# Values held and probabilities streamed in the last two attentions of a two-block transformer kernel

## The chip, the cores and the metric

The kernel runs on one core of one Trainium2 chip. The metric is the device time of one execution in microseconds. Engines are named as in the profile: PE multiplies matrices (PEld loads its stationary operand), DVE, ACT and POOL work on vectors, SP only issues transfers.

## What is computed

The reference applies two transformer blocks to 256 tokens of width 1024, in float32. The first has a dilated attention and a dense causal one, 8 heads each, and a feed-forward part. The second has two layers: a sparse attention of 16 heads (a compressed, a selected and a window branch, each with a gate per token and head), then an attention over key blocks of 16 heads; each layer ends in a mixture of 32 experts and a gated embedding. With 256 tokens all keys are in reach, so selected and window branch are two causal attentions with a linear bias. What the change touches, cut from the reference:

```python
o_s = jnp.einsum('bgrqnl,bgqnld->bgrqd', p_s.astype(v_g.dtype), v_g)
...
o_w = jnp.einsum('bgrqk,bgkd->bgrqd', p_w.astype(vwc.dtype), vwc)
o = gc[..., 0:1] * o_c + gc[..., 1:2] * o_s + gc[..., 2:3] * o_w
...
return o @ w_out
```

```python
pr = jax.nn.softmax(sc, axis=-1)
...
o = (jnp.einsum('bgrqkl,bgrqkld->bgrqd', p_sel, v_g)
     + jnp.einsum('bgrql,bgld->bgrqd', p_own, vo))
return o.transpose(0, 3, 1, 2, 4).reshape(b, MOBA_Q_BLOCK, ATT_DIM)
...
h = h + mix.astype(h.dtype)
```

## The kernel before

The program is written engine by engine: each engine has one list of instructions in an order set by hand, and semaphores join them. Nothing reorders. Weights come through `ring`, eight slots of 512 KB filled by SP; each chunk is split into a high part (a cast on ACT) and a low part (a subtraction on DVE) in `weight_parts` (four of them, `PAIRS`), and a product is three matmuls per chunk and tile: high x high, high x low, low x high (`pe_linear`, L881). An input of such a product is first turned by PE (`pe_turn`, L787), then rounded by ACT into `x_high` and subtracted by DVE into `x_low`.

There are four attentions. The first, `att_a` (8 heads, from about 98 us), and the second, `att_b`, belong to block one. The third, `att_n`, holds 32 heads (for each of four key groups four heads on selected keys, gate 1, then the same four on window keys, gate 2, whose result is added); the fourth, `att_m`, 16 heads. One head has two query tiles: 128 queries against 128 keys, 128 queries against 256 keys, side by side in 384 columns (`SPAN`). Its way:

- scores on PE (`scores_of_four`, L975, four heads at a time, two heads at once on row halves) into banks 0 to 3;
- bias and negated maximum on DVE (L1080, two instructions and two short reads) into `logit`, exponentials with their sum on ACT (L1044) into `prob`, four buffers;
- three transposes on PE (`turn_probs`, L985) into bank 4 or 5, a copy to `probT` (ACT L1053 for even heads, DVE L1089 for odd ones), two buffers;
- values on PE (L996): `probT` is held, 128 columns of values are streamed, three times;
- for four heads, DVE takes the reciprocal of the sums (L1100), multiplies by the gate (L1103), scales the values from the banks into `mix` (L1108) and adds where the core has `add` (L1111).

In the third attention a compressed branch runs along: DVE shifts its scores (`dve_shift_compressed`, L1179 to L1184), ACT exponentiates, DVE weighs (L1193 to L1201), PE turns it at the end and multiplies with `own_values` (L1160) and DVE adds into `mix` (L1208). After each of these two attentions `mix` is turned, split, and multiplied by the output weights (`l_nsa_o`, `l_moba_o`). POOL scales some queries and keys (L950) and clears halves of the turned keys (`clear_keys`, L2004), for which PE waits.

## Time and profile before

| | us |
|---|---|
| median of three runs | 1079.68 (1078.15 to 1079.87) |
| the profiled execution | 1079.15 |
| its span in the profile | 1077.4 |
| third attention, first score to its output projection | 57.39 |
| fourth attention, the same | 28.17 |

What stands outside the span in the profiled execution is 1.75 us. The page of the profile gives each engine's busy share; a window query gives the same for a stretch, and the timeline lists instructions with the idle time before them and what ended it.

### The profile page before, as it was taken

Reading aid. Unit: us, or ns where it says so; the run is one execution under the profiler, and the core shown is the slowest. Engines: PE = TensorE matmul, PEld = TensorE weight load, DVE = VectorE, ACT = ScalarE, POOL = GpSimd, SP = SyncE. Lnnn points to the kernel's source line nnn. Section 1 sums busy time; section 2 is a strip of 40 time slices with the busy share of each in tenths; the row PEclk is TensorE's granted clock in tenths of the full one; section 3 lists DMA queues with packets and bytes.
Section 4 is the critical chain, followed back from the end, with each engine's and each line's share of the span. In section 5 each row is a group of like instructions: output and inputs, shape, how many; then the busy total and the mean of one; then the engine's idle time right before and its main releaser. Section 6 shows DMA issues by size and latency. Waiting matters only on the chain.

```text
span 1077.4 us, 17463 instructions
## 1 busy us (share of the span) xinstructions
PE 1022.7 (95%) x6136; PEld 854.6 (79%) x6136; DVE 766.3 (71%) x1347; ACT 700.9 (65%) x1201; POOL 104.0 (10%) x189
## 2 busy tenths in 40 slices
PE   7998899999998999799999999999989999999998
PEld 6876788999997877787687778767878688778766
DVE  4686557666666667777668788787766768888876
ACT  5665545434445536575588898957666578899955
POOL 9008000000000101000320000000010240000000
PEclk9998999999999999999999999999999999999999
DMA  9871028566654555004439999854324428999950
GB/s 295 287 238 56 1 84 246 181 188 180 193 175 162 157 192 200 1 2 156 176 119 327 332 339 339 305 194 147 127 79 152 180 69 326 336 333 339 334 181 40
DMA packets 106156, 209.25 MB, mean 194 GB/s; under 512 B 7736, under 2 KB 51744, under 8 KB 105824
## 3 DMA queue, kind: packets, MB, share of 16 engines
q1 hardware_dynamic: 103584, 204.04, 55.6%
q0 software_dynamic: 2064, 3.25, 1.1%
q8 instruction: 43, 0.70, 0.3%
q10 hardware_dynamic: 432, 0.99, 0.3%
q14 instruction: 33, 0.27, 0.1%
HBM read 207.19 MB, written 1.06 MB: 193 GB/s over the span
## 4 chain that ended last, share of the span: by engine, by line
PE 83%; DVE 7%; ACT 5%; issue 2%; POOL 2%; DMA 1%; SPq 0%; ACTq 0%; DVEq 0%; POOLq 0%
PE bank L881 21%; PE bank L1638 18%; PE bank L1657 11%; PE bank L1311 8%; PE bank L1321 8%; PE bank L996 4%; PE bank L985 2%; PE bank L975 2%; PE bank L787 2%; PE bank L1679 1%; PE bank L1506 1%; DMA ring<-in_a_w_in 1%; PE bank L1649 1%; PE bank L1468 1%; PE bank L2161 1%
## 5 line engine op out<-in xcount | busy, mean ns | idle before, releaser
L881 PE MATMUL bank<-weight_parts,x_high 128*128 128x512 f32 (+2 forms) x768 | 224.1, 376 | 8.6 <-ACT x_high L851 2.6
L1638 PE MATMUL bank<-expert_high,block_high 128*128 128x256 f32 x560 | 183.4, 328 | 3.3 <-ACT block_low L1586 2.4
L1566 DVE TENSOR_TENSOR expert_low<-expert_w,expert_high 128x1024 fp32r<-128x1024 f32 x140 | 164.6, 1218 | 10.6 <-ACT expert_high L1559 10.4
L881 PEld LDWEIGHTS bank<-weight_parts,x_high 128*128 128x128 f32 x768 | 140.0, 189 | 35.8 <-ACT x_high L851 6.9
L1638 PE MATMUL bank<-expert_high,block_low 128*128 128x256 f32 x560 | 158.1, 282 | 0.0
L902 DVE TENSOR_TENSOR weight_parts<-ring,weight_parts 128x1024 fp32r<-128x1024 f32 (+3 forms) x112 | 121.2, 1103 | 51.7 <-ACT weight_parts L899 51.0
L1638 PE MATMUL bank<-expert_low,block_high 128*128 128x256 f32 x560 | 158.0, 282 | 0.0
L899 ACT CAST weight_parts<-ring 128x1024 fp32r<-128x1024 f32 (+3 forms) x112 | 104.3, 956 | 77.5 <-PE bank L881 58.3
L1559 ACT CAST expert_high<-expert_w 128x1024 fp32r<-128x1024 f32 x140 | 140.1, 1053 | 18.9 <-DMA expert_w<-in_moe_w_up 18.4
L881 PE MATMUL bank<-weight_parts,x_low 128*128 128x512 f32 (+2 forms) x384 | 143.6, 374 | 0.0
L1657 PE MATMUL bank<-expert_w,junk 128*128 128x512 f32 x280 | 131.2, 592 | 0.0
L1638 PEld LDWEIGHTS bank<-expert_high,block_high 128*128 128x128 f32 x560 | 106.8, 191 | 20.4 <-issue 14.3
L1638 PEld LDWEIGHTS bank<-expert_low,block_high 128*128 128x128 f32 x560 | 106.9, 191 | 14.7 <-issue 14.7
L1638 PEld LDWEIGHTS bank<-expert_high,block_low 128*128 128x128 f32 x560 | 106.8, 191 | 0.0
L1311 PE MATMUL bank<-x_high,parts 128*128 128x256 f32 x512 | 97.5, 283 | 0.4 <-DVE x_low L853 0.3
L1321 PE MATMUL bank<-parts,hid_parts 128*128 128x512 f32 x384 | 92.9, 391 | 0.0
L1713 DVE SCALAR_TENSOR_TENSOR arena<-bank,home_w,arena 128x1024 f32 x64 | 82.2, 1284 | 9.3 <-issue 5.6
L1311 PEld LDWEIGHTS bank<-x_high,parts 128*128 128x128 f32 x512 | 82.1, 191 | 2.2 <-issue 0.7
L881 PEld LDWEIGHTS bank<-weight_parts,x_low 128*128 128x128 f32 x384 | 72.4, 189 | 12.8
L1321 PEld LDWEIGHTS bank<-parts,hid_parts 128*128 128x128 f32 x384 | 70.1, 188 | 13.3
L1657 PEld LDWEIGHTS bank<-expert_w,junk 128*128 128x128 f32 x280 | 47.7, 190 | 34.4 <-issue 34.3
L1584 ACT CAST block_high<-sorted_high 128x1024 fp32r (+1 forms) x70 | 73.4, 1051 | 1.8 <-issue 1.0
(357 smaller groups left out, 1699.9 us busy)
## 6 DMA issues: line engine op xcount, KB each, us to landing
expert_w<-in_moe_w_gate SPq DMA_DIRECT2D x70, 512.0 KB, 5.9
expert_w<-in_moe_w_up SPq DMA_DIRECT2D x70, 512.0 KB, 7.3
expert_w<-in_moe_w_down SPq DMA_DIRECT2D x70, 512.0 KB, 5.5
ring<-in_w_ff SPq DMA_DIRECT2D x64, 512.0 KB, 3.9
ring<-in_w_in SPq DMA_DIRECT2D x16, 512.0 KB, 8.7
ring<-in_a_w_in SPq DMA_DIRECT2D x16, 512.0 KB, 6.5
ring<-in_ple_w_gate SPq DMA_DIRECT2D x16, 512.0 KB, 5.5
ring<-in_w_o SPq DMA_DIRECT2D x8, 512.0 KB, 4.1
```

Source lines behind the costliest of these rows:

```text
L881: mm = nc.tensor.matmul(bank[:, j["m"] % 4, 0:n], j["operand"][x][:, 2 * c + kk, at[0]:at[1]], weight_parts[:, number % PAIRS, w, kk * n:( ...
L899: nc.scalar.copy(high, raw_weights).then_inc(weights_high, 1)
L902: nc.vector.tensor_tensor(low, raw_weights, high, ALU.subtract).then_inc(weights_split, 1)
L996: mm = nc.tensor.matmul(bank[:, 6 + t, (n % 4) * P:(n % 4 + 1) * P], probT[:, n % 2, q * P:(q + 1) * P], v[:, kt, at - 64:at + 64], start= ...
L1311: mm = nc.tensor.matmul(bank[:, b, 0:256], parts[:, u % 2, w, k * P:(k + 1) * P], x[:, k, :], start=k == 0 and n == 0, stop=k == KB - 1 an ...
L1321: mm = nc.tensor.matmul(bank[:, 2 * t + half, :], hid_parts[:, u % 2, x, t * P:(t + 1) * P], parts[:, u % 2, w, 2048 + half * 512:2048 + ( ...
L1559: nc.scalar.copy(half_of(expert_high[:, b % 2, :], j), half_of(expert_w[:, b % DEPTH, 0:2048], j)).then_inc(ex_cast, 1)
L1566: nc.vector.tensor_tensor(half_of(expert_low[:, b % DEPTH, 0:2048], j), half_of(expert_w[:, b % DEPTH, 0:2048], j), half_of(expert_high[:, ...
L1584: nc.scalar.copy(block_high[:, b % 2], sorted_high[:, :, ds(at, P)]).then_inc(ex_copied, 1)
L1638: mm = nc.tensor.matmul(bank[:, 4 + b % 2, 0:256].rearrange("p (q n) -> p q n", q=2), x[:, b % 2, k, :], w[:, k], start=k == 0 and n == 0, ...
L1657: mm = nc.tensor.matmul(bank[:, 2 * (b % 2) + half, :], hidTs[:, b % 2, :], expert_w[:, b % DEPTH, 2048 + half * 512:2048 + (half + 1) * 5 ...
L1713: v.scalar_tensor_tensor(out=here, in0=bank[:, 2 * (b % 2):2 * (b % 2) + 2, :].rearrange("p b n -> p (b n)"), scalar=share_of, in1=here, o ...
```

## The change

- In the last two attentions the shares (reciprocal of the sum, times gate) are made per pair of heads, and POOL multiplies the probabilities by them, in place, before they are turned.
- `values` now holds 64 columns of values and streams `probT` (256 and 128 columns); two heads write the two halves of the partitions of one bank, which is then one chunk of the mixed rows, already turned. Selected and window branch of a pair accumulate in the same bank, the compressed branch is added there by two more matmuls (`joined`).
- ACT rounds a finished pair into `x_high`, DVE subtracts into `mixed_low`; the turns of `mix` and the additions after the loop go. The output weights are read in the matching row order (`rows_by_chunk`).
- `probT` has four buffers. The first splits of the output weights move into the last group of heads.
- In the first attention the turn of queries and keys moves into `l_va`, ahead of its third chunk, and DVE's two roots behind its copy of `l_va`; in the third, DVE spreads `own_values` before it takes the compressed scores; ahead of the fourth, `l_v`'s splits move ahead of root and scaling, and half of the queries is turned inside `l_v`.
- POOL no longer clears halves of turned keys.
- SP's transfer of the embedding weights waits for the last pair instead of the last mix.

```diff
                 c = chunk(lambda x: x[:, 0:2 * width].rearrange("p (k n) -> p k n", k=2),
-                          w.rearrange("(p k) n -> p k n", k=k)[:, kp:kp + 2, c0:c0 + width], 1,
+                          w.rearrange("(k p) n -> p k n" if rows_by_chunk else "(p k) n -> p k n", k=k)[
+                              :, kp:kp + 2, c0:c0 + width], 1,
                           (weights_split, number + 1))
...
-    t_mix2 = turn(mix, KB, [(x_high, None, x_low)])
-    l_nsa_o = linear(a["a_w_out_2"][0], KB, D_MODEL, x_parts, h, "add")
+    l_nsa_o = linear(a["a_w_out_2"][0], KB, D_MODEL, mixed_parts, h, "add", rows_by_chunk=True)
...
             for c, number in enumerate(group[0]["splits"]):
+                if turn_ahead is not None and group[0] is jobs[0] and c == 2:
+                    pe_turn(pe, turn_ahead)
                 if turned_by and group[0] is jobs[0]:
                     wait_turned(pe, turned_by[c:c + 1])
+                if pairs_mixed is not None and group[0] is jobs[0]:
+                    pe.wait_ge(pair_mixed, pairs_mixed + 2 * c + 2)
...
+    def pe_pairs(pe, s, compressed=False):
+
+        first, here, count = s["first"], s["heads"], len(s["heads"])
+        pairs = pairs_of(s)
+
+        def turn_probs(j):
+            n = first + j
+            pe.wait_ge(weighed, s["first_weighed"] + j + 1)
+            if j >= 2:
+                pe.wait_ge(*probT_of(n - 2))
+            if compressed and j == 6:
+                pe.wait_ge(cT_ready, 1)
+            for q in range(3):
+                mm = nc.tensor.transpose(bank[:, 4 + n % 2, q * P:(q + 1) * P], prob[:, n % 4, q * P:(q + 1) * P],
+                                         ident)
+            mm.then_inc(probs_turned, 1)
...
+        def values(m):
+            x = pairs[m]
+            n = first + 2 * m
+            for i in range(2):
+                pe.wait_ge(*probT_of(n + i))
+            if x["opens"] and x["freed"]:
+                pe.wait_ge(pair_mixed, x["freed"])
+            joined = compressed and x["closes"]
+            for kt, lo, hi in ((0, 0, 2 * P), (1, 2 * P, 3 * P)):
+                for i, head in enumerate(x["heads"]):
+                    v, at = head["v"]
+                    mm = nc.tensor.matmul(bank[64 * i:64 * i + 64, x["bank"], P * kt:2 * P], v[:, kt, at:at + 64],
+                                          probT[:, (n + i) % 4, lo:hi], start=x["opens"] and kt == 0,
+                                          stop=x["closes"] and kt == 1 and not joined, skip_group_check=True)
+            if joined:
+                half = x["chunk"] // 4
+                cols = slice(x["chunk"] % 4 * P, x["chunk"] % 4 * P + P)
+                for t in range(TILES):
+                    mm = nc.tensor.matmul(bank[:, x["bank"], t * P:(t + 1) * P], own_values[:, half, cols],
+                                          cT[:, 2 * half + t, :], start=False, stop=t == 1, skip_group_check=True)
+            mm.then_inc(pair_made, 1)
+
+        scores_of_four(pe, first, here[0:4])
+        if compressed:
+            pe.wait_ge(c_scored, KV_HEADS)
+        for j in range(0, count, 4):
+            if j + 4 < count:
+                scores_of_four(pe, first + j + 4, here[j + 4:j + 8])
+            turn_probs(j)
+            turn_probs(j + 1)
+            if j:
+                values(j // 2 - 1)
+            if compressed and j == 4:
                 pe_turn_compressed(pe)
-            values(first + j, here[j])
+            turn_probs(j + 2)
+            turn_probs(j + 3)
+            values(j // 2)
+        values(count // 2 - 1)
+
...
+    def act_pairs(act, s, weights, compressed=False):
+
+        first, count = s["first"], len(s["heads"])
+        pairs = pairs_of(s)
+
+        def take_probs(j):
+            n = first + j
+            act.wait_ge(probs_turned, n + 1)
+            if j >= 4:
+                act.wait_ge(pair_made, s["first_pair"] + (j - 4) // 2 + 1)
+            nc.scalar.copy(probT[:, n % 4, :], bank[:, 4 + n % 2, 0:SPAN]).then_inc(act_probT, 1)
+
+        def high(m):
+            x = pairs[m]
+            if x["closes"]:
+                act.wait_ge(pair_made, x["m"] + 1)
+                nc.scalar.copy(x_high[:, x["chunk"], :], bank[:, x["bank"], 0:TOKENS]).then_inc(pair_high, 1)
+
...
+            take_probs(j)
+            if not last:
+                exps_of(act, first + j + 4)
+            if compressed and j == 0:
+                act.wait_ge(c_shifted, 1)
+                nc.scalar.activation(cl[:, :, :, :], cl[:, :, :, :], ACT.Exp).then_inc(c_exped, 1)
+            if j:
+                high(j // 2 - 1)
+            if compressed and j == 4:
+                act_compressed(act)
+            take_probs(j + 2)
+            if last:
+                split_first(act, weights, "act", 0, 1)
+            else:
+                exps_of(act, first + j + 5)
+            high(j // 2)
+            if last:
+                split_first(act, weights, "act", 1, 2)
+            else:
+                exps_of(act, first + j + 6)
+                exps_of(act, first + j + 7)
+        high(count // 2 - 1)
+        split_first(act, weights, "act", 2, 3)
+        act.wait_ge(pair_made, pairs[-1]["m"] + 1)
+        split_first(act, weights, "act", 3)
+
...
+        pairs = pairs_of(s)
+
+        def bias(j):
+            if j < count:
+                bias_head(dve, first + j, here[j])
+
+        def shares(m):
+            if 0 <= m < len(pairs):
+                n = first + 2 * m
+                here_shares = head_share[:, n % 4:n % 4 + 2, :]
+                dve.wait_ge(probs_made, n + 2)
+                by_head = total[:, n // 4 % 2, :].rearrange("p (t h) -> p h t", t=TILES)[:, n % 4:n % 4 + 2, :]
+                ins = nc.vector.reciprocal(here_shares, by_head)
+                if pairs[m]["gate"] is not None:
+                    dve_link(dve, ins)
+                    head = here[2 * m]["head"]
+                    ins = nc.vector.tensor_tensor(here_shares, here_shares, gates[:, :, head:head + 2, pairs[m]["gate"]]
+                                                  .rearrange("p t h -> p h t"), ALU.mult)
+                ins.then_inc(share_ready, 1)
+
+        def take_probs(j):
+            n = first + j
+            dve.wait_ge(probs_turned, n + 1)
+            if j >= 4:
+                dve.wait_ge(pair_made, s["first_pair"] + (j - 4) // 2 + 1)
+            nc.vector.tensor_copy(probT[:, n % 4, :], bank[:, 4 + n % 2, 0:SPAN]).then_inc(dve_probT, 1)
+
+        def low(m):
+            x = pairs[m]
+            if x["closes"]:
+                dve.wait_ge(pair_high, x["taken"])
+                nc.vector.tensor_tensor(mixed_low[:, x["chunk"], :], bank[:, x["bank"], 0:TOKENS],
+                                        x_high[:, x["chunk"], :], ALU.subtract).then_inc(pair_mixed, 1)
+
+        for j in range(4):
+            bias(j)
+        shares(0)
+        if compressed:
+            dve_shift_compressed(dve)
+        for j in range(0, count, 4):
+            last = j + 4 == count
+            bias(j + 4)
+            shares(j // 2 + 1)
+            take_probs(j + 1)
+            bias(j + 5)
+            if last:
+                split_first(dve, weights, "dve", 0, 1)
+            if j:
+                low(j // 2 - 1)
+            bias(j + 6)
+            take_probs(j + 3)
+            bias(j + 7)
+            shares(j // 2 + 2)
+            if last:
+                split_first(dve, weights, "dve", 1, 2)
+            low(j // 2)
+            if compressed and j == 0:
+                dve_weigh_compressed(dve)
+        low(count // 2 - 1)
+        split_first(dve, weights, "dve", 2)
+
+    def pool_weigh(pool, s):
+
+        for j in range(len(s["heads"])):
+            n = s["first"] + j
+            pool.wait_ge(share_ready, s["first_pair"] + j // 2 + 1)
+            for t, (lo, hi) in enumerate(((0, P), (P, SPAN))):
+                here = prob[:, n % 4, lo:hi]
+                last = nc.gpsimd.tensor_tensor(here, here, head_share[:, n % 4, t:t + 1].to_broadcast([P, hi - lo]),
+                                               ALU.mult)
+            last.then_inc(weighed, 1)
...
-            last_of_pair = max(n for n in l_g[0]["splits"] if n % PAIRS == pair)
-            pool.wait_ge(lin_made, splits[last_of_pair]["made"])
-            clear_keys(keys)
+        pool_weigh(pool, att_n)
         pool_clear_acc(pool, 0)
         pool_steps(pool, 0)
         pool.wait_ge(scale_ready, 8)
         scale_heads(g, mk, scales(r_mk, 0, 4), pool_scaled)
-        pool.wait_ge(pool_scaled, 5)
...
-        pe_linear(pe, l_va)
         pe.wait_ge(dve_scaled, 2)
-        pe_turn(pe, t_a)
+        pe_linear(pe, l_va, turn_ahead=t_a)
         wait_turned(pe, t_a)
         wait_took(pe, l_va)
-        pe.wait_ge(keys_cleared, 2)
         pe_attention(pe, att_a, by_four=True)
...
         pe_turn(pe, t_kv)
         pe_linear(pe, l_q[2:4])
         pe_linear(pe, l_k, t_kv)
-        pe_linear(pe, l_v)
-        for g in range(2):
-            pe.wait_ge(dve_scaled, 4 + g)
-            pe_turn(pe, t_mq[g])
+        pe.wait_ge(dve_scaled, 4)
+        pe_linear(pe, l_v, turn_ahead=t_mq[0])
+        pe.wait_ge(dve_scaled, 5)
+        pe_turn(pe, t_mq[1])
         pe.wait_ge(pool_scaled, 5)
         pe_turn(pe, t_mk)
         wait_turned(pe, t_mk + t_mq[0] + t_mq[1])
         wait_took(pe, l_v)
-        pe.wait_ge(keys_cleared, 8)
-        pe_attention(pe, att_m, by_four=True)
-        pe.wait_ge(mixed, n_heads[0] // 4)
-        pe_turn(pe, t_mix3)
-        pe_linear(pe, l_moba_o, t_mix3)
+        pe_pairs(pe, att_m)
+        pe_linear(pe, l_moba_o, pairs_mixed=KB)
         pe_moe_and_ple(pe, 1)
...
+        take_turn(dve, t_a, "dve")
         dve_latent_sums(dve)
+        take_linear(dve, l_va, "dve")
         dve_root(dve, r_bq, scale_ready)
         dve_root(dve, r_bk, scale_ready)
-        take_linear(dve, l_va, "dve")
-        take_turn(dve, t_a, "dve")
         dve.wait_ge(toep_ready, 32)
         dve_attention(dve, att_a, by_four=True)
         take_turn(dve, t_b, "dve")
...
+            else:
+                take_linear(dve, l_k, "dve")
             dve_root(dve, r_mq[g], scale_ready)
             dve.wait_ge(scale_ready, 6 + g)
             steepen(r_mq[g], 8 * g, 8)
             scale_heads(v, mq[:, :, 8 * g:8 * g + 8, :], scales(r_mq[g], 0, 8), dve_scaled)
-        take_linear(dve, l_k, "dve")
         dve.wait_ge(squared, 9)
         v.tensor_reduce(r_mk["sum"], work[:, 0:512].rearrange("p (h d) -> p h d", d=64), AX.X,
                         ALU.add).then_inc(sums_ready, 1)
```

How the instructions stand on three places. DVE at the first attention, before: the copy of l_va (L930), the turns' copies, then the first bias; the roots (L744 to L749) stand ahead of these rows.

```order
L748 TENSOR_SCALAR stat<-stat 128x16 [waits dve_step]
L749 TENSOR_TENSOR stat<-stat 128x16 [waits dve_step]
L930 TENSOR_SCALAR arena<-bank,stat 128x512 [waits rooted,lin_made]
L832 TENSOR_SCALAR ring<-bank,head_gain 128x512 [waits turned]
L820 TENSOR_SCALAR ring<-bank,head_gain 64x512 [waits turned] x2
L1080 ISA work,neg_max<-bank,toep 128x128 [waits scores_made,toep_ready]
```

The same place after: the turns' copies come first, then the sums, the copy of l_va (L938), and the twelve steps of the two roots (the first five stand here, the other seven follow up to the first bias).

```order
L836 TENSOR_SCALAR ring<-bank,head_gain 128x512 [waits turned]
L824 TENSOR_SCALAR ring<-bank,head_gain 64x512 [waits turned] x2
L1253 TENSOR_REDUCE stat<-mix 128x2 [waits squared]
L1255 TENSOR_REDUCE stat<-rows 128x16
L1258 TENSOR_TENSOR stat<-stat 128x16 [waits dve_step]
L938 TENSOR_SCALAR arena<-bank,stat 128x512 [waits rooted,lin_made,sums_ready]
L748 RECIPROCAL stat<-stat 128x16 [waits roots_taken]
L749 TENSOR_SCALAR stat<-stat 128x16 [waits dve_step]
L750 TENSOR_TENSOR stat<-stat 128x16 [waits dve_step]
L751 TENSOR_TENSOR stat<-stat 128x16 [waits dve_step]
L752 TENSOR_SCALAR stat<-stat 128x16 [waits dve_step]
```

The roots moved from ahead of the copy to behind it. DVE in the third attention, before: a copy of turned probabilities, one bias (four rows), and the shares and the mix of four heads.

```order
L1089 COPY probT<-bank 128x384 [waits values_made,probs_turned]
L1080 ISA work,neg_max<-bank,table 128x128 [waits probs_made,scores_made]
L1080 ISA neg_max 128x1
L1080 ISA work,neg_max<-bank,table 128x256
L1080 ISA neg_max 128x1
L1100 RECIPROCAL share<-total 128x8 [waits probs_made]
L1103 TENSOR_TENSOR share<-share,gates 128x8 [waits mix_step]
L1108 TENSOR_TENSOR part<-bank,share 128x512 [waits values_made,mix_step]
L1111 TENSOR_TENSOR mix<-mix,part 128x2x256 [waits mixed]
```

After: the shares of a pair stand between a bias and the copy of an odd head; POOL waits for them (`share_ready`), and PE's transposes for POOL (`weighed`).

```order
L1188 RECIPROCAL head_share<-total 128x4 [waits probs_made]
L1192 TENSOR_TENSOR head_share<-head_share,gates 128x4 [waits dve_step]
L1201 COPY probT<-bank 128x384 [waits pair_made,probs_turned]
L1168 ISA work,neg_max<-bank,table 128x128 [waits probs_made,scores_made]
L1168 ISA neg_max 128x1
L1168 ISA work,neg_max<-bank,table 128x256
L1168 ISA neg_max 128x1
L1207 TENSOR_TENSOR mixed_low<-bank,x_high 128x256 [waits pair_high]
```

The mix of four heads is gone from DVE, and shares and the subtraction of a pair came in. DVE ahead of the fourth attention, before: scaling of the second half of the queries, then the four splits for `l_v`.

```order
L950 TENSOR_TENSOR arena<-arena,stat 128x512 [waits dve_step]
L950 TENSOR_TENSOR arena<-arena,stat 128x512
L902 TENSOR_TENSOR weight_parts<-ring,weight_parts 128x512 [waits weights_high] x4
L930 TENSOR_SCALAR arena<-bank,stat 128x256 [waits rooted,lin_made]
L2607 TENSOR_REDUCE stat<-work 128x8 [waits squared]
```

After, the splits and the copy of `l_k` stand right behind the sums, ahead of the root.

```order
L2716 TENSOR_REDUCE stat<-rows 128x16 [waits squared]
L910 TENSOR_TENSOR weight_parts<-ring,weight_parts 128x512 [waits weights_high] x4
L938 TENSOR_SCALAR arena<-bank,stat 128x256 [waits rooted,lin_made]
L748 RECIPROCAL stat<-stat 128x16 [waits roots_taken]
L749 TENSOR_SCALAR stat<-stat 128x16 [waits dve_step]
```

The four splits moved past the six steps of the root, one multiplication and the scaling.

## Rows read from the trace of the kernel before

**Rows 1.** The page: busy us, share of the span, instructions, by engine.
```profile
PE 1022.7 (95%) x6136; PEld 854.6 (79%) x6136; DVE 766.3 (71%) x1347; ACT 700.9 (65%) x1201; POOL 104.0 (10%) x189
```

**Rows 2.** Windows: stretch, its us, busy PE PEld DVE ACT POOL (x), PEclk, DMA, GB/s.
```profile
436.48:493.87 57.39, 51.91 (x445) 45.00 (x445) 46.80 (x190) 39.11 (x150) 0.00 (x0) 1.00 0.06 20
793.26:821.43 28.17, 25.36 (x224) 22.62 (x225) 18.91 (x83) 20.12 (x76) 0.00 (x0) 1.00 0.05 11
```

**Rows 3.** Timeline, PE, third attention: start us, us, engine, line, op, tiles [idle before].
```profile
451.99 0.49 PE L985 MATMUL bank<-table,work 128*128 128x128 f32 x3
...
454.08 1.58 PE L975 MATMUL bank<-ring 64*128 64x128 f32 x16
455.59 0.55 PE L985 MATMUL bank<-table,work 128*128 128x128 f32 x3
455.98 0.83 PE L996 MATMUL bank<-arena,probT 128*128 128x128 f32 x6
...
459.74 1.58 PE L975 MATMUL bank<-ring 64*128 64x128 f32 x16
```

**Rows 4.** Timeline, DVE, the same stretch.
```profile
452.52 0.56 DVE L1089 COPY probT<-bank 128x384 f32<-128x384 f32 x1 [0.33 <-PE bank L985]
453.00 0.28 DVE L1080 CUSTOM_DVE_ANT_0 work<-bank,table 128x128 f32<-128x128 f32 x1
...
453.55 0.20 DVE L1100 RECIPROCAL share<-total 128x8 f32<-128x8 f32 x1
453.78 0.17 DVE L1103 TENSOR_TENSOR share<-share,gates 128x8 f32<-128x8 f32 x1
```

**Rows 5.** Timeline, multiplications on POOL elsewhere, and a subtraction on DVE.
```profile
82.24 1.32 POOL L2037 TENSOR_TENSOR rows<-arena,rope 128x128 f32<-128x128 f32 x1
100.28 5.75 POOL L950 TENSOR_TENSOR arena<-arena,stat 128x768 f32<-128x768 f32 x4
539.96 0.40 POOL L1797 TENSOR_TENSOR probT<-routes,bounds 128x128 f32<-128x128 f32 x1
787.44 1.18 POOL L950 TENSOR_TENSOR arena<-arena,stat 128x256 f32<-128x256 f32 x2 [236.69 <-DVE stat L749]
...
81.83 1.42 DVE L902 TENSOR_TENSOR weight_parts<-ring,weight_parts 128x1024 fp32r<-128x1024 f32 x1
```

**Rows 6.** Timeline, start of the fourth attention, PE, DVE and ACT.
```profile
793.26 1.58 PE L975 MATMUL bank<-ring 64*128 64x128 f32 x16 [1.67 <-ACT ring L809]
795.91 0.55 PE L985 MATMUL bank<-table,work 128*128 128x128 f32 x3 [1.06 <-ACT work L1044]
...
794.19 0.29 DVE L1080 CUSTOM_DVE_ANT_0 work<-bank,table 128x128 f32<-128x128 f32 x1 [1.03 <-PE bank L975]
...
794.87 0.40 ACT L1044 ACTIVATE work<-work,neg_max 128x128 f32<-128x128 f32 x1 [1.73 <-DVE neg_max L1080]
...
795.76 0.39 ACT L1044 ACTIVATE work<-work,neg_max 128x128 f32<-128x128 f32 x1
```

**Rows 7.** Windows, DVE alone: compressed shift and compressed weighing of the third attention.
```profile
439.72:441.86 2.14, 2.07 (x7) 1.00 0.00 0
444.78:447.75 2.97, 2.80 (x9) 1.00 0.00 0
```

**Rows 8.** Timeline, PE: first scores of the third attention; first matmuls of l_v.
```profile
436.48 1.58 PE L975 MATMUL bank<-ring 64*128 64x128 f32 x16 [1.74 <-issue]
...
782.03 0.80 PE L881 MATMUL bank<-weight_parts,kv_high 128*128 128x256 f32 x2 [2.72 <-DVE weight_parts L902]
```

**Rows 9.** Timeline, PE: first scores of the first attention; window, DVE: its two roots.
```profile
97.78 1.74 PE L975 MATMUL bank<-ring 64*128 64x128 f32 x16 [2.25 <-POOL ring L2004]
...
89.15:92.42 3.27, 2.87 (x12) 1.00 0.00 0
```

**Rows 10.** Windows, PE alone: busy (x), granted clock, DMA share, GB/s.
```profile
435.00:450.00 15.00, 9.65 (x88) 1.00 0.00 1
783.00:784.00 1.00, 1.00 (x7) 0.50 0.67 106
```

243 lines of the change are left out of this document (95 added, 148 removed).

## The prediction

> **What bounds the kernel now.** I read the page's busy shares first: PE 95% of the span, DVE 71%, ACT 65%, POOL 10% [rows 1]. So PE sets nearly everything, and PE work that is taken away shows in the end, unless the stretch it is taken from turns out to be bound by something else. Then the stretches that the change rewrites, by the busy time in a window: the third attention, from its first score to the first matmul of its output projection, takes 57.39 us, of which PE is busy 51.91, DVE 39.11 and POOL 0.00; the fourth takes 28.17 us with PE busy 25.36 [rows 2] (in these rows the columns are PE, PE's loads, DVE, ACT, POOL). Third, PE's own order in time: four heads cost 1.51 us of scores (454.08 to 455.59), then each head 0.33 of transposes and 0.67 of values, and the next four begin 5.66 us later (459.74) [rows 3]. 1.51 + 4 x 1.00 = 5.51, so PE is the bound of this loop and nothing else is near. The question is what bounds it when PE has less to do.
>
> **Part 1, PE's work in the loop.** A head's values were three streams of 128 columns, 0.67 us. Now a pair of heads streams 256 + 128 columns each, side by side on column halves. If the halves overlap, a pair costs about what one head cost: 0.67; if not, 1.34. No row shows column halves. The nearest is the scores on row halves: four heads stream 4 x 384 columns in 1.51 us, where 384 columns of values alone take 0.67 [rows 3], so pairs overlapped almost wholly (1.51 against 2.68). I take 0.70 and keep 1.34 for the range. PE then needs 1.51 + 4 x 0.33 + 2 x 0.70 = 4.2 us for four heads in place of 5.5, in the third attention 0.45 more in a mean group for the compressed values, which come inside.
> The Trainium skill, page "TensorEngine Tiling (Array Packing)", section "Tiling Modes", says that column tiles work independently, which agrees, and that changing the tiling mode drains the engine. The first transposes after scores show 0.55 beside 0.49 for the others [rows 3], so a drain is some 0.06 us; by that rule the four more switches in a group cost 0.25 us of PE, which has 1.9 us to spare.
>
> **Part 2, the new round through POOL.** Weighing puts two POOL multiplications per head, 128x128 and 128x256, between exponential and transposes. POOL's rows: 0.40 us for 128x128 with a broadcast operand, 1.18 for two of 128x256 [rows 5]. A head costs 0.36 + 0.58 = 0.94 to 1.01, I take 0.97; four heads 3.9. That alone is under 5.66. But POOL cannot run on from group to group. The first pair of the next group gets its shares on DVE only after DVE has copied the last head's turned probabilities and made one more bias, and that head is turned only after POOL weighed it. From transposes to transposes: 0.53 to DVE's copy (451.99 to 452.52), 0.47 copy, 0.55 bias, 0.23 + 0.17 shares and gate [rows 3, 4], 0.13 to reach POOL (a bias starts at 794.19, its exponential at 794.87, of which 0.55 is the bias [rows 6]), 3.9 weighing, 0.15 back to PE: **6.1 us**, and 5.9 without the gate.
> A second round holds where a pair closes: transposes, values 0.33 + 0.70 + 0.25 until ACT can round the pair, 0.45 until DVE can subtract, 0.34 subtraction (estimates between a 0.40 us step of ACT and a 0.56 us copy of 384 columns [rows 4, 6]), two biases and a copy 1.57, shares 0.36, two heads 1.94, 0.15: 6.1. With gate and joined compressed values 6.7.
> So a group takes 6.1 in the fourth attention, and in the third 6.1 and 6.7 by turns, 6.4. Both are above 5.66: **the loop gets slower although PE's part shrinks by a quarter.** Bounds: 5.9 to 6.9.
>
> **Part 3, the fourth attention as a sum.** Until the fourth head is turned: 0.93 to the bias, 0.68 to the exponential, 0.89 for the first head's, 1.04 for the second's [rows 6], shares 0.36, POOL 3.9, 0.15: 7.9. Three groups at 6.1: 18.3. Then the tail. The transposes of mix, the wait ahead of them and the wait for the split are gone, but in the last group DVE's first weight subtraction stands ahead of its copy of the last head, and waits for ACT's cast: from the last head's transposes 3.2 us until its values can start, 0.7 for these: 3.9. In all 30.1, bounds 29.5 to 32.5, against 28.17: +2.0.
> It begins earlier. PE stood idle 2.72 us ahead of 782.03 for the weight parts of l_v, which DVE made after the scaling of the queries [rows 8]; DVE now makes them first, and the turn of half the queries fills PE inside l_v. DVE then carries shift, root, scaling and the turns' copies in a row and ends 2.3 us before it did. Sum for the fourth: -0.3.
>
> **Part 4, the third attention.** Until the fourth head is turned: as above, with shares 0.43, then DVE's compressed shift of 2.14 [rows 7] now ahead of the fifth bias, bias 0.55, shares 0.54, two heads 1.94, 0.15: 9.3. The next group carries the compressed weighing, 2.97 [rows 7], on the same round: 8.1. Six groups at 6.4: 38.4. Tail 4.0. Sum 59.8 against 57.39. The copy, bias and exponential stretches are covered by each other as before; compressed values and their addition, once after the loop, have cover now.
> Here DVE and POOL meet. A POOL multiplication at 82.24 took 1.32 us, where its kind takes 0.40, and a DVE subtraction of two SBUF tiles (1.42 us from 81.83) stood beside it [rows 5]. At 100.28 four POOL steps of 768 columns took 5.75 us amid biases, in line with 256 columns, so biases don't disturb [rows 5]. Shift and weighing of the compressed part are of the first kind and meet the weighing of four heads: I take +0.8, bounds 0 and 2. The start is 1.7 us earlier, since PE's idle 1.74 us ahead of 436.48 [rows 8] waited for own_values, which DVE now spreads first. Sum: 60.6 - 57.4 - 1.7 = +1.5.
> The Trainium skill, page "SBUF — State Buffer", section "Who interferes with whom", says that a DVE instruction with two SBUF inputs and a GpSimd one that reads SBUF exclude each other for a whole instruction. The rows at 81.83 and 82.24 agree. By it every gate multiplication under a running weighing would wait up to 0.6 us too; off the round in part 2, so the sum stays.
>
> **Part 5, the first attention.** POOL's clearing of keys, for which PE idled 2.25 us ahead of 97.78, goes, and the turns move into l_va. But DVE's twelve steps of two roots, 3.27 us in this profile [rows 9], which lay under l_va, now stand between l_va's copy (ends about 96.3) and the first bias, where POOL's 512-column steps stand beside them. First bias then 99.0 to 100 in place of 98.7 (97.78 + 0.93): +0.6, bounds 0 and +1.5.
>
> **Sum.** +0.6 + 1.5 - 0.3 = +1.8; 0.4 more for mode switches and shorter clock. The profiled execution took 1079.15, the median is 1079.68: no difference that matters, so **1081.9 us**. The output projections themselves, loads and the ring keep their cost: weights stood ready before.
>
> **Rivals.**
> *The weighing is hidden (faster).* If POOL's round does not bind, ACT does: four heads' exponentials 3.6, two copies 0.7, rounding 0.3 to 0.6: 4.9 a group. Third -7.5, fourth -4.0, first +0.6: 1069. It decides where a POOL head takes under about 0.85 us: then the round falls under 5.66 and the gain of the two earlier starts (4.0) is kept, 1076. For it: POOL is idle now and PE's part shrinks. Against: 0.94 at the least by rows. Chance 0.20 for all of it, most near 1076.
> *A wash.* Rounds at their lower bound and no collision: third -0.1, fourth -0.9, first 0: 1078.7; up to the forecast's low side. Chance 0.33.
> *Column halves do not overlap.* A pair costs 1.34: closing rounds 6.75 and 7.3, tails +0.65: third +4.8, fourth +1.8, first +0.6: 1086.9. It would be seen at once in PE's rows. Chance 0.10.
> *POOL slower than its rows.* Heads of 1.1 us from collisions or the broadcast: 12 groups x 0.5: 1087. Chance 0.10.
> *PE's clock falls.* PE is busy two thirds of the loop. It kept 1.00 through 15 us with 9.65 busy, but after 2.72 us idle it ran at 0.50 [rows 10], with 1.2 instead of 2.4 GHz. Idle pieces here are about 1 us. If all ran at half, a group takes 8.6: +28. Chance 0.04, single episodes more, +1 each.
>
> **How the numbers follow.** The forecast itself, slower by 2 to 5 us, has 0.23. A measurement of this kernel can tell about 0.2%, 2.2 us, from no change. Faster 0.20; same 0.35, which takes the wash and the forecast's low edge; slower 0.45: forecast 0.21, the three slow rivals 0.24. Both signs hold chance, so the likeliest case's own range is 1079 to 1085; the range for 8 in 10 is 1075 to 1089.
>
> **What would show it.** POOL's weighing at 0.36 and 0.58 us, busy about 46 us, idle 2.2 us a group with DVE's shares as releaser. PE waiting ahead of transposes for POOL. Groups of scores 6.1 to 6.7 us apart. First bias of the first attention at 99 or later; first scores of the third at 434.8 on the old clock. Pairs of values at 0.7 a pair. I am wrong if groups come under 5.7 us apart, or PE shows 1.3 a pair.

## The result

The changed kernel took 1081.88 us (median of 20 runs, 1079.67 to 1088.77), the kernel before beside it 1079.14 (20 runs, 1077.02 to 1080.05). The ratio is 1.0035, with a 95% interval of 1.0025 to 1.0045: slower by 0.35%, or 3.8 us (the two medians are 2.7 apart, the two means 3.5). The profiled execution took 1080.27 (span 1078.5), against 1079.15 (1077.4) before, so the pair of traces shows 1.1 us of the difference and the rest lies in how the executions spread: here before stays within 3.0 us and the changed kernel reaches over 9. In the later rounds before spread by 4.7 to 6.9.

Three words are used below. A group is four heads of an attention; groups follow each other in the loop. A round is a chain of waits that closes over the loop, from one step of a group to the same step of the next. The tail is an attention from its last group of scores to the first matmul of its output projection.

The page of the changed kernel, in the columns of [rows 1], and then the windows that answer to [rows 2], in their columns:

```profile
PE 1015.1 (94%) x6032; PEld 831.4 (77%) x6032; DVE 757.6 (70%) x1355; ACT 704.4 (65%) x1209; POOL 143.5 (13%) x277
```
```profile
433.41:494.11 60.70, 50.50 (x389) 33.67 (x389) 42.48 (x197) 41.28 (x155) 31.52 (x64) 0.92 0.01 1
791.45:821.61 30.16, 21.75 (x177) 13.79 (x177) 19.48 (x89) 22.52 (x81) 15.09 (x32) 0.98 0.00 1
```

PE's busy time is 7.6 us less and the kernel got longer: in both windows PE's idle time grew (5.5 to 10.2 and 2.8 to 8.4) by more than its work shrank. What took its place is seen in the fourth attention, POOL first (idle time ahead, and who ended it), then PE at the same time, then DVE:

```profile
800.89 3.86 POOL L1244 TENSOR_TENSOR work<-work,head_share 128x128 f32<-128x128 f32 x8 [1.92 <-DVE head_share L1188]
806.81 1.33 POOL L1244 TENSOR_TENSOR work<-work,head_share 128x128 f32<-128x128 f32 x3 [2.06 <-DVE head_share L1188]
```
```profile
794.74 1.58 PE L974 MATMUL bank<-ring 64*128 64x128 f32 x16 [1.71 <-DVE neg_max L1168]
...
800.77 1.58 PE L974 MATMUL bank<-ring 64*128 64x128 f32 x16 [0.40 <-DVE neg_max L1168]
...
820.13 1.55 PE L1069 MATMUL bank<-probT,arena 128*64 128x256 f32 x8 [2.24 <-DVE probT L1201]
821.61 1.22 PE L889 MATMUL bank<-weight_parts,x_high 128*128 128x512 f32 x2
```
```profile
805.53 0.55 DVE L1201 COPY probT<-bank 128x384 f32<-128x384 f32 x1
...
806.55 0.18 DVE L1188 RECIPROCAL head_share<-total 128x4 f32<-128x4 f32 x1
```

POOL weighs four heads in 3.86 (ends 804.75), DVE copies the last head (805.53), makes a bias, then the shares (806.55), and POOL goes on at 806.81: a round of 5.92, in which POOL stands idle for 2.06 us.

To see where the time of the whole program went, five traces are cut at the same places (PE's start of the named work; the last three kernels are experiments, below). Us:

| stage, up to | before | changed | first attention's edit alone | starts alone | reordered and moved |
|---|---|---|---|---|---|
| first turn for the second attention | 115.04 | 115.96 | 115.77 | 113.08 | 112.50 |
| first score of the third | 321.44 | 317.45 | 321.40 | 317.53 | 317.45 |
| third attention | 57.39 | 60.70 | 57.38 | 58.77 | 54.76 |
| first score of the fourth | 299.39 | 297.34 | 300.86 | 297.98 | 298.25 |
| fourth attention | 28.17 | 30.16 | 28.17 | 29.05 | 25.22 |
| end of the span | 255.97 | 256.89 | 257.22 | 255.99 | 256.02 |
| median, and ratio to before | | 1081.88, 1.0035 | 1081.38, 1.0024 | 1073.73, 0.9958 | 1065.67, 0.9879 |

Changed against before: +0.9, -4.0, +3.3, -2.1, +2.0, +0.9 = +1.1. Granted clock enters several cells: windows of PE with its clock (busy, count, clock, DMA) at the same places, of before, then of the kernel with the starts alone, then of the changed one.

```profile
99.00:107.00 8.00, 6.98 (x41) 0.57 0.01 2
430.00:434.00 4.00, 4.00 (x23) 0.57 0.02 4
```
```profile
99.00:107.00 8.00, 6.72 (x65) 1.00 0.01 2
430.00:434.00 4.00, 2.71 (x26) 1.00 0.00 0
```
```profile
437.00:448.00 11.00, 10.04 (x53) 0.54 0.00 1
820.00:824.00 4.00, 3.87 (x15) 0.57 0.18 23
```

Before had a stretch at 1.2 in place of 2.4 GHz at 99 to 106 and one in its compressed scores at 430 to 434, which took 5.44 us in place of 3.81. Of the 4.0 between the turns and the third attention 1.6 is therefore clock. The compressed scores in the traces of before and of the starts alone:

```profile
429.31 5.44 PE L1145 MATMUL bank<-kcT,ring 128*128 128x128 f32 x32 [0.31 <-DVE ring L832]
```
```profile
426.87 3.81 PE L1147 MATMUL bank<-kcT,ring 128*128 128x128 f32 x32 [0.31 <-DVE ring L832]
```

The changed kernel had its own at 437 to 448 and at 820, where its output projection begins: that one is the +0.9 at the end.

### The profile page after: what moved, and what is told of

Read it like the earlier page. It is cut to its first block, busy times and chain, and to the rows that moved or that the text cites. A ratio compares the mean times of both kernels' runs of the same rounds, so it can differ in the third digit from the quotient of the medians.

```text
span 1078.5 us, 17318 instructions
## 1 busy us (share of the span) xinstructions
PE 1015.1 (94%) x6032; PEld 831.4 (77%) x6032; DVE 757.6 (70%) x1355; ACT 704.4 (65%) x1209; POOL 143.5 (13%) x277
## 4 chain that ended last, share of the span: by engine, by line
PE 80%; DVE 8%; ACT 5%; issue 3%; POOL 2%; DMA 1%; ACTq 0%; SPq 0%; DVEq 0%; POOLq 0%
PE bank L889 23%; PE bank L1809 17%; PE bank L1828 11%; PE bank L1482 8%; PE bank L1492 8%; POOL work L1244 1%; PE bank L791 1%; PE bank L2311 1%; PE bank L974 1%; PE bank L1004 1%; DVE work L1168 1%; PE bank L1850 1%; PE bank L1054 1%; PE bank L1677 1%; PE bank L1069 1%
## 5 line engine op out<-in xcount | busy, mean ns | idle before, releaser
L889 PE MATMUL bank<-weight_parts,x_low 128*128 128x512 f32 (+2 forms) x320 | 118.8, 371 | 0.0
L1809 PEld LDWEIGHTS bank<-expert_low,block_high 128*128 128x128 f32 x560 | 106.8, 191 | 15.3 <-issue 15.3
L1482 PE MATMUL bank<-x_low,parts 128*128 128x256 f32 x256 | 72.4, 283 | 0.0
```

The source lines that it names most:

```text
L889: mm = nc.tensor.matmul(bank[:, j["m"] % 4, 0:n], j["operand"][x][:, 2 * c + kk, at[0]:at[1]], weight_parts[:, number % PAIRS, w, kk * n:( ...
L1482: mm = nc.tensor.matmul(bank[:, b, 0:256], parts[:, u % 2, w, k * P:(k + 1) * P], x[:, k, :], start=k == 0 and n == 0, stop=k == KB - 1 an ...
L1809: mm = nc.tensor.matmul(bank[:, 4 + b % 2, 0:256].rearrange("p (q n) -> p q n", q=2), x[:, b % 2, k, :], w[:, k], start=k == 0 and n == 0, ...
```

## Experiments

**1. The same kernel again.**

> The changed kernel as it is, for a second trace and more times. Its profiled execution was only 1.1 us longer than the one of before, while its median was 2.7 longer, and its longer executions show a lower mean granted clock (0.977 to 0.983 where the short ones show 0.985 to 0.991). Theory 'clock': the floor stays 1.1 to 1.3 us over before, and some executions have stretches at half clock in a place where PE is dense; 0.005 to 0.01 of 1080 us at half clock is 5 to 10 us, worth up to half of it in time, 3 to 6 us: executions at 1083 to 1089. If this trace is of a long one, the stretch shows in its windows. Rival 'waits': the long executions have the same clock by stages, and their extra time lies in PE's idle time ahead of transposes, spread over the groups of the third attention.

Measured 1082.12 (1079.00 to 1087.82, 12 runs; before 1078.20), ratio 1.0036 [1.0021, 1.0051]. The two longest executions had a mean granted clock of 0.979 and 0.983, the two shortest 0.988; before's were at 0.989 to 0.994. This trace, of 1082.17, was not of a long one: third attention 60.39, fourth 30.05. So these two stages repeat within 0.3. The start doesn't: the first turn for the second attention stood at 117.79, 1.8 later than in the first trace, and that is nearly all of the 1.9 by which this span is longer. Over the eight traces that hold this start unchanged it stood at 114.24 to 117.79. The place of the long executions' extra time was open until experiment 6.

**2. Shares ahead of the copy.**

```
             bias(j + 6)
+            shares(j // 2 + 2)
             take_probs(j + 3)
             bias(j + 7)
-            shares(j // 2 + 2)
```

> One line moved: DVE makes the shares of the next group's first pair ahead of the copy of the last head's turned probabilities and of the last bias, in place of behind both. Theory 'one round' (as the prediction costs it: transposes, copy, bias, shares, POOL): copy 0.47 and bias 0.55 leave the round, POOL's idle stretch of 1.92 to 2.06 us a group shrinks by 1.0, groups 5.1 apart in the fourth attention and 5.4 to 5.7 in the third: 3 groups x 1.0 + 7 x 1.0 = -10, about 1071. Rival 'rounds in a row': the shares need the exponential of head j+5, which ACT makes only behind its copy of head j+2; DVE then stands still (about 0.6 us: 806.1 against 805.53 in the trace) with that copy behind it, so the pair's values, its rounding and the next bias come later by that much, and the gain goes: groups 6.0 to 6.4 as before, 1080 to 1083. Third: POOL's duration binds (it has no idle time left after this edit) and its rows show 4 x 0.97.

Measured 1088.34, ratio 1.0086 [1.0070, 1.0101]: slower still. POOL, then PE, then DVE's shares, in the fourth attention:

```profile
803.88 1.90 POOL L1244 TENSOR_TENSOR work<-work,head_share 128x128 f32<-128x128 f32 x4 [1.36 <-DVE head_share L1188]
806.62 1.90 POOL L1244 TENSOR_TENSOR work<-work,head_share 128x128 f32<-128x128 f32 x4 [0.84 <-DVE head_share L1188]
```
```profile
804.85 1.58 PE L974 MATMUL bank<-ring 64*128 64x128 f32 x16 [0.92 <-DVE neg_max L1168]
...
811.18 1.03 PE L974 MATMUL bank<-ring 64*128 64x128 f32 x10 [1.26 <-DVE neg_max L1168]
```
```profile
803.62 0.18 DVE L1188 RECIPROCAL head_share<-total 128x4 f32<-128x4 f32 x1 [0.66 <-ACT work L1103]
```

POOL's one idle piece of 2.0 became two (1.36 and 0.84, in the next group 1.68 and 0.85), and groups of scores stand 6.33 to 6.56 apart in place of 5.92 to 6.03, in the third attention 6.55 to 7.04. DVE now waits for ACT's exponential (0.66) with the copy and the last bias behind it, and PE's next scores wait for that bias. The theory of one round falls: another round, through ACT's exponentials and DVE, is as long or longer once this one is cut. The other rival, rounds in a row, gave the mechanism, but its 1083 fits only the trace, of the shortest execution (1082.45); the others, at 1085 to 1089, had a mean clock of 0.980 to 0.986.

**3. Another order of the same work.** ACT makes two exponentials in a row, and DVE three biases around its first copy, with the shares behind the last bias:

```
 ACT  copy j, exp j+4, [+exp j+5], high, copy j+2, [-exp j+5], exp j+6, high, exp j+7
-DVE  bias 4, shares, copy 1, bias 5, low, bias 6, copy 3, bias 7, shares, low
+DVE  bias 4, shares, bias 5, copy 1, bias 6, bias 7, shares, low, copy 3, low
 in the last group: DVE's first two split_first behind copy 3
```

> Same work, other order in the two pair loops. ACT: exponentials of heads j+4 and j+5 one after the other behind the copy of head j, then rounding, copy j+2, exponential j+6, rounding, exponential j+7. DVE: bias j+4, shares, bias j+5, copy j+1, biases j+6 and j+7, shares of the next group's first pair, subtraction, copy j+3, subtraction; in the last group both first weight subtractions stand behind the copies. Theory 'order of the rounds': POOL's weighing is covered and what is left is near ACT's 4.9 us or DVE's 4.5 a group plus one handover, groups 5.1 to 5.7 apart: 3 x 0.6 + 1.7 (tail) = -3 to -4.5 in the fourth, 7 x 0.7 + 1.7 = -6 to -8 in the third, in all 1070 (1067 to 1073), POOL idle under 1.3 us a group. Rival 'POOL and DVE hinder each other' (or POOL's own pace is the bound): weighing spread over more DVE work grows above 0.97 a head, groups stay at 6, only the tails go: 1078. Rival 'clock': groups as short as theory says, but the median stays over 1075 with a mean granted clock under 0.985.

Measured 1070.18 (1068.12 to 1071.52), ratio 0.9917 [0.9902, 0.9932]: as the theory said. Third 54.67 (groups 5.21 and 5.88 by turns), fourth 26.26. POOL's idle pieces are 0.4 to 1.1 a pair, and its heads still take 0.95 (1.90 for two): its own pace was not the bound. No work was taken away, so 12 us of the changed kernel's time were order. More of it stands at the tails than in the loops: of the 9.9 by which the two attentions are shorter in the traces, 6.2 are the tails (15.3 to 12.4 and 14.9 to 11.7 us), 2.5 of which the moved weight splits give by themselves (experiment 5), and 3.7 the groups before.

**4. POOL's work cut by 60%.** The kernel leaves out the weighing of columns 128 to 383 of every head.

```
-            for t, (lo, hi) in enumerate(((0, P), (P, SPAN))):
+            for t, (lo, hi) in enumerate(((0, P),)):
```

> The changed kernel with one of POOL's two weighings of each head left out (columns 128 to 383 are not weighed, which is left out of the computation): a head costs POOL 0.37 in place of 0.96. Prices POOL's own time in the round. Theory 'one round through POOL': the round of 6.0 holds four heads, 4 x 0.59 = 2.4 less would make it 3.7, so the next bound shows: ACT's 4.9 or the pair-closing round, which holds two heads and loses 1.2: 4.8 to 5.3 a group in the fourth attention, 5.0 to 5.5 in the third: 3 x 0.9 + 7 x 1.1 + 1.2 twice for the start = -12, 1070. That would bound what the prediction's faster rival (weighing hidden, 1069) could have been. Rival 'the order binds, not POOL': waits of DVE and ACT on each other hold the group at 5.8 or more, and it is 1078.

Measured 1073.71, ratio 0.9952 [0.9937, 0.9968], between the two. A head costs POOL 0.38, and PE's groups of scores still stand up to 6.3 us apart:

```profile
455.96 1.58 PE L974 MATMUL bank<-ring 64*128 64x128 f32 x16 [1.09 <-DVE neg_max L1168]
...
461.32 1.58 PE L974 MATMUL bank<-ring 64*128 64x128 f32 x16
...
467.65 1.58 PE L974 MATMUL bank<-ring 64*128 64x128 f32 x16 [1.04 <-DVE neg_max L1168]
```

5.36 and 6.33 by turns (6.19 and 6.58 with whole weighing), and 5.16 and 5.80 in the fourth attention. In the third, the group in which pairs close moved by only 0.25: DVE waits there 0.67 for ACT's exponential (463.59) and 0.60 for its rounding (465.59), POOL stands idle for 1.79 and more, and PE's scores wait for DVE's bias. Taking 2.3 us a group off POOL brought the mean group of the third attention to 5.85, reordering with POOL's whole work to 5.55. The larger gain of the order in the medians, 3.5 us, is mostly the tails (12.4 and 11.7 against 13.9 and 13.6 here, where the weight splits stand as in the changed kernel). This kernel is faster than before, though: POOL's time does decide the sign, together with the order.

**5. The tail.**

```
-            if last:
-                split_first(dve, weights, "dve", 0, 1)
             if j:
                 low(j // 2 - 1)
             bias(j + 6)
             take_probs(j + 3)
+            if last:
+                split_first(dve, weights, "dve", 0, 1)
```

> The changed kernel, one statement moved in the last group of each pair loop: DVE's first weight subtraction stands behind its copy of the last head's turned probabilities, in place of ahead of the subtraction, the bias and this copy. PE's idle time of 2.24 us ahead of the last pair's values (820.13, released by that copy) and of 1.31 in the third attention. Theory (part 3's tail): the copy no longer waits for ACT's cast and 1.1 us of subtraction, the last values start 1.5 to 2 us earlier, and the weight part is still ready in time for the first matmul: third -1.4, fourth -1.7 against the changed kernel's 60.5 and 30.1, in all -3: 1079. Rival: the first matmul then waits for the weight part or for the last pair's low part in its place, and the stages shorten by under 0.5 each: 1081.

Measured 1079.23 (12 runs), ratio 1.0006 [0.9993, 1.0020], where the changed kernel stood at 1.0035 and 1.0036: 3 us, as expected. Third 58.67 (-1.9 against the mean of two traces), fourth 29.03 (-1.1). The tail itself is 1.4 shorter in the third and 1.1 in the fourth; the other 0.6 of the third stand in its first groups, where this trace has a shorter stretch at half clock. PE at the end of the fourth attention, where 820.13 above had waited 2.24:

```profile
816.80 1.64 PE L1069 MATMUL bank<-probT,arena 128*64 128x256 f32 x16
819.36 0.70 PE L889 MATMUL bank<-weight_parts,x_high 128*128 128x512 f32 x2 [0.92 <-issue]
```

The wait ahead of the values is gone, and 0.92 of it came back ahead of the projection: the theory holds, with a part of what the rival said.

**6. The column halves in turn.**

```
-            for kt, lo, hi in ((0, 0, 2 * P), (1, 2 * P, 3 * P)):
-                for i, head in enumerate(x["heads"]):
+            for i, head in enumerate(x["heads"]):
+                for kt, lo, hi in ((0, 0, 2 * P), (1, 2 * P, 3 * P)):
```

> The changed kernel with the four matmuls of a pair of values in another order: both of head i (256 and 128 columns) on its column half, then both of head i+1 on the other, in place of by turns. Nothing is left out. Theory: PE runs what stands next in line, and only neighbours on different halves overlap: 256 alone, then 128 beside 256 of the other half, then 128: 512 to 640 columns in place of 384: a pair takes 1.05 to 1.2 in place of 0.80. The round in which a pair closes grows by 0.3 to 0.4, the other (through the last head's copy) does not contain values: fourth +0.3 x 3 and the tail 0.3, third +0.3 x 3 (every second group) and the tail: +2 to +2.5 over the changed kernel (1082.1). Rival (prediction's): no overlap at all, 1.34 a pair. Rival 2: the halves run as if apart, whatever the order: 0.80 and no change.

Measured 1083.02 (1079.36 to 1088.67), ratio 1.0035 [1.0018, 1.0053], no change. A pair of values, first of the changed kernel, then of this one:

```profile
462.60 0.87 PE L1069 MATMUL bank<-probT,arena 128*64 128x256 f32 x8
463.40 0.55 PE L1054 MATMUL bank<-table,work 128*128 128x128 f32 x3
```
```profile
456.95 0.88 PE L1069 MATMUL bank<-probT,arena 128*64 128x256 f32 x8
457.76 0.49 PE L1076 MATMUL bank<-toep,ring 128*128 128x128 f32 x2
```

0.80 and 0.81 to the next work, in either order, where one head alone took 0.67 before [rows 3]. My theory of neighbours falls; the second rival holds: the halves overlap, and the order of the four matmuls doesn't matter. This trace is also of one of the long executions (1085.96). Its windows on PE, and PE's rows at the fourth attention's tail:

```profile
488.00:492.00 4.00, 3.60 (x18) 0.56 0.02 6
492.00:496.00 4.00, 3.95 (x23) 0.59 0.00 0
...
816.00:820.00 4.00, 3.85 (x19) 0.57 0.00 0
820.00:823.00 3.00, 1.08 (x11) 1.00 0.01 3
823.00:827.00 4.00, 3.43 (x13) 0.50 0.02 6
827.00:830.00 3.00, 3.00 (x9) 0.53 0.90 336
```
```profile
816.02 1.83 PE L1054 MATMUL bank<-table,work 128*128 128x128 f32 x6 [1.79 <-POOL work L1244]
...
823.57 1.55 PE L1069 MATMUL bank<-probT,arena 128*64 128x256 f32 x8 [2.48 <-DVE probT L1201]
```

The last groups of both attentions and the first 5 us of the projection behind the fourth ran at 1.2 GHz, in the third after PE had been idle for 1.80 us, in the fourth for 1.79 and for 2.48. The same idle piece of the third stood in the first trace of the changed kernel (1.81, ahead of 486.73), and there the tail ran at full clock:

```profile
484.00:496.00 12.00, 8.45 (x62) 5.85 (x61) 6.43 (x18) 7.21 (x20) 3.78 (x8) 1.00 0.01 3
```

So such a piece can be followed by half clock, and isn't in every execution. The span is 5.7 longer than the changed kernel's first trace: 1.5 ahead of the third attention (half clock in its compressed scores), 1.1 in the third (61.79), 1.2 in the fourth (31.35), 2.3 behind it, and 0.3 less between. So most of this long execution's extra time lies at the two tails; it is the only long one with a trace.

**7. PE kept busy.**

```
+            filler(n, 8 if j == 0 else 2)       # transposes of ident, ahead of
             pe.wait_ge(weighed, ...)            # each head; 12 behind the first scores
```

> The changed kernel with idle PE filled in its two pair loops: 12 transposes of a constant behind the first scores, 8 ahead of the first head's transposes and 2 ahead of every other's, into the bank that the next transposes overwrite (0.11 us each at full clock, by 0.33 for three; 0.22 a head, 0.9 a group, where PE stands idle 1.4 to 1.8 us a group). Nothing is left out. Theory 'clock': the executions of 1083 to 1089 come from stretches at half clock that PE's idle pieces in these loops bring about; with the idle filled, granted clock 1.00 through both loops, the half-clock stretch at 437 to 449 gone (third attention 60.7 to about 59), mean clock over 0.988 in all executions and their spread down to 3 us as before's, median 1078 to 1080. Rival 'waits': spread and median stay (1082, up to 1088), a little longer for up to 0.2 us more at each wait. Rival 'no control over it': half clock comes at the same place in spite of a busy PE.

Measured 1081.18 (1077.61 to 1083.84, 12 runs), ratio 1.0024 [1.0010, 1.0038]. Both attentions at full clock:

```profile
433.26:494.18 60.92, 53.54 (x472) 40.38 (x471) 42.59 (x197) 41.67 (x155) 31.52 (x64) 1.00 0.01 1
791.12:821.45 30.33, 25.36 (x227) 19.02 (x227) 18.85 (x88) 22.40 (x81) 15.11 (x32) 1.00 0.00 1
```

Mean clock 0.989 to 0.995, where the changed kernel's executions had 0.977 to 0.991, and no execution over 1084: the theory holds in that half clock in these loops comes with the idle pieces. That the executions of 1085 to 1089 are gone with it is likely and not certain: 9 of the 44 executions without fillers took over 1085 (experiments 1 and 6 counted in), and at that rate 12 without one come about by chance about once in sixteen times. The expected median of 1078 to 1080 was missed: the fillers' own cost ate the gain in the stages (groups of 6.12 to 6.25 in the fourth, in place of 5.92 to 6.03; third attention 60.92, expected about 59). The spread is still 6.2 us, but before beside it spread by 6.9, so no part of it need belong to the change.

**8 and 9. One part alone.** The kernel before with the edit of the first attention, and the kernel before with the two earlier starts; ACT's and DVE's copies of the turns that moved go along with them:

```
 a_only        pe_linear(l_va, turn_ahead=t_a); roots behind take_linear(l_va); no clear_keys(kaT)
 starts_only   own values first; take_linear(l_k) ahead of the 2nd root; turn_ahead=t_mq[0]; no clear_keys
```

> The kernel before with the change's edits of the first attention alone: turns inside l_va, DVE's roots behind its copy of l_va, no clearing of the keys on POOL there. Theory (the traces: first transposes 6.2 us behind the end of l_va against 4.9 with turns between; one root step of 16 columns took 1.19 us beside POOL, at 97.46): the first bias comes 1.3 later, +1.3, and PE's idle 3.6 us ahead of the first transposes is followed by 3.4 us at half clock, up to 1.5 more where before has none: 1079.5 to 1081 against 1078.2. Prediction's term: +0.6. Rival: half clock falls there in executions of before as well, so that only the idle time tells: +1.3 or less, and the two earlier moves (turns, clearing) pay it back: 0 to +0.5.

> The kernel before with only the change's earlier starts of the third and fourth attention: own values spread ahead of taking the compressed scores; the splits of l_v made ahead of the second scaling, half the queries turned inside l_v; no clearing of the keys on POOL for these two. Attentions, turns of the mix and projections as before, and the first attention as before. Theory (parts 3 and 4 of the prediction): third 1.7 earlier, fourth 2.3 earlier, all of it kept to the end since each attention runs at its own pace: -4.0, 1075. Rival: what waits moves on (ACT or the values' spread is next in line): the two starts are worth 0.5 to 2 together, 1077 to 1079.

The first measured 1081.38, ratio 1.0024 [1.0012, 1.0036], +2.6 us. DVE there, as in the changed kernel:

```profile
97.26 1.19 DVE L746 TENSOR_TENSOR stat<-stat 128x16 f32<-128x16 f32 x1
98.49 0.18 DVE L747 TENSOR_TENSOR stat<-stat 128x16 f32<-128x16 f32 x1
...
100.24 0.29 DVE L1082 CUSTOM_DVE_ANT_0 work<-bank,toep 128x128 f32<-128x128 f32 x1
```
```profile
95.93 2.49 POOL L2057 TENSOR_TENSOR arena<-second,gain_bk 128x512 f32<-128x512 f32 x2
```

A product of 16 columns took 1.19 us beside POOL's second multiplication of 512 columns, its neighbour 0.18. The first bias came at 100.24, in the kernel with the starts alone at 99.17, although there the turns stood between. PE then waited 3.53 us ahead of its first transposes, and a stretch at half clock followed at 102. The trace is of one of the longer executions (1082.55) and doesn't place the 2.6: of the 3.4 by which its span exceeds before's, only 0.7 stand in the first stage, 1.5 between the third and the fourth attention and 1.3 behind the fourth, where nothing was edited. Against the kernel with the starts alone, which kept before's start and had it at full clock, the first stage is 2.7 longer.

The second measured 1073.73, ratio 0.9958 [0.9942, 0.9974], -4.5 against the expected -4.0. Its trace is 5.0 shorter than before's, by stages: -2.0 in the first, which it doesn't touch (before's half clock), -3.9, +1.4, -1.4, +0.9 and 0.0. The +1.4 and the +0.9 stand in the unedited attentions, where this trace has stretches at half clock and before's has none.

**10. The roots back under l_va,** on top of the order of 3.

```
-        take_linear(dve, l_va, "dve")
         dve_root(dve, r_bq, scale_ready)
         dve_root(dve, r_bk, scale_ready)
+        take_linear(dve, l_va, "dve")
```

> The reordered kernel (1070.2) with the first attention's start put back: DVE's two roots ahead of its copy of l_va, as before; turns still inside l_va, and POOL still doesn't clear the keys. Theory (part 5, and 6.2 us from the end of l_va to the first transposes where before with its turn behind it had 4.9): the twelve small steps return under l_va, first transposes 1.3 us or more earlier, and with the two gains (no wait for clearing, turn inside) up to 3: 1068.5 (1067 to 1069.5). Rival: the copy of l_va then comes 3.3 us later, since it waits in DVE's line behind the roots, and PE waits for that copy: 1070 to 1072.

Measured 1069.06, ratio 0.9908 [0.9885, 0.9930] against 0.9917 of the order alone: inconclusive, the intervals overlap. In the traces the first stage is 1.9 shorter (113.96 for 115.83). Theory and rival both showed: two root steps took 1.28 and 1.19 under POOL, the copy of l_va came at 97.33 in place of 96.02, and PE's wait moved from the transposes (3.54 to 0.56) to the scores (0.99 to 3.93).

**11. The roots inside the loop, and PE's order.**

```
 dve_attention(att_a): + dve_root(r_bq) behind the 4th bias, dve_root(r_bk) behind the 6th
 pe_pairs:               turn_probs(j + 2)
                       + values(j // 2)
                         turn_probs(j + 3)
                       - values(j // 2)
```

> The reordered kernel (1070.2) with two more moves: DVE's two roots of the second attention stand inside the first attention's loop, behind its 4th and its 6th bias, with no root ahead of the first bias; and PE streams a pair's values ahead of the last head's transposes in each group. Theory: the first bias follows scores by 0.93 (first transposes about 99.7 in place of 102.0), two of the 2.3 us kept, since six small steps of 0.2 us fit into DVE's free time of 1.7 a group: -1 to -2. Pairs close 0.5 earlier in the closing round: groups near 5.0 to 5.6: -1 to -2. In all 1067 (1066 to 1068.5). Rival: the roots delay the 5th and 7th bias on which ACT waits and POOL's scaling comes later, the gain of the first attention is under 0.5; ACT's line binds the loops, and the order of PE brings nothing: 1069.5.

Measured 1065.67 (1064.44 to 1067.76, 5 runs; before 1078.33), ratio 0.9879 [0.9857, 0.9901]. It beats both kernels, by 12.7 and by 16 us, and by more than I expected. First transposes at 99.57 in place of 102.16; fourth attention 25.22; third 54.76, with groups at

```profile
456.06 1.58 PE L974 MATMUL bank<-ring 64*128 64x128 f32 x16
...
461.42 1.58 PE L974 MATMUL bank<-ring 64*128 64x128 f32 x16
...
466.78 1.58 PE L974 MATMUL bank<-ring 64*128 64x128 f32 x16
```

5.36 apart. The two moves weren't run apart, but the traces tell most of it. Against the order alone the first stage is 3.3 shorter (112.50 for 115.83), the third attention 0.1 longer, the fourth 1.0 shorter, of which 0.9 is half clock in the other kernel's first scores. So the gain is that of the roots, and PE's order brought little that shows.

**12. The same with fillers at the starts.** Transposes of a constant in `pe_pairs`: 12 behind the first scores, and 8 ahead of the transposes of heads 0, 4, 6 and 8 in the third attention and of head 0 in the fourth, behind the waits for the buffers and ahead of the wait for POOL.

> As the kernel with the moved roots and PE's order, and PE kept busy where the third attention falls to half clock (437 to 448 in the traces) and at the start of the fourth: 12 transposes of a constant behind the first scores, 8 ahead of the transposes of heads 0, 4, 6 and 8 of the third and of head 0 of the fourth. Theory 'clock': the first three groups of the third attention run at full clock; where PE binds there (third group 8.6 in the reordered kernel) 1 to 2 us come back: 1 to 2 under the kernel without them, 1065.5. Rival: the groups there wait for DVE's compressed steps (2.14 and 2.97), not for PE, and the fillers' 0.9 us stand in the way of the transposes: same or +1.

Measured 1070.96, ratio 0.9924 [0.9904, 0.9944]: 5 us worse. The half clock of the first three groups shrank from 6.8 us to 3.4, at 449, but PE there waits for the compressed branch (2.36 us, for ACT's copy of its turned product) and then has much to do at once, and each row of fillers stood ahead of it:

```profile
447.74 1.06 PE L1048 MATMUL bank<-table 128*128 128x128 f32 x8 [2.36 <-ACT toep L1350]
448.64 0.49 PE L1060 MATMUL bank<-table,work 128*128 128x128 f32 x3
449.06 1.55 PE L1075 MATMUL bank<-probT,arena 128*64 128x256 f32 x8
```

The fillers came behind the wait for the compressed copy, not under it, and the clock fell all the same. Third 57.04 in place of 54.76, fourth 26.06 in place of 25.22, and 1.8 more behind it, where no filler stands. The rival was right, and its price was too small.

## The prediction, point by point

- **What bounds the loop.** Right: POOL's round, with DVE's shares as releaser, 5.92 to 6.03 by the trace where 6.1 was summed, in the third attention 6.19 and 6.58 by turns for 6.1 and 6.7. Right by more luck than the sum tells: I treated the two rounds as two limits of which the longer counts. Experiments 2 and 4 show further waits of DVE and ACT for each other close behind, so that neither edit gained what its round's sum says; how many rounds there are, and how long each is, stays open. The faster rival put its point of decision at a POOL head of 0.85. No run stands there; at 0.38 the kernel was faster than before by 5 us, but the mean group of the third attention was 5.85, still over the 5.66 under which the rival wanted it, so POOL alone wouldn't have brought the rival's gain in the loop. Its neighbour, *POOL slower than its rows*, adds 12 x 0.5 to 1081.9, which is 1087.9 and not 1087.
- **The pair of values.** 0.80 for the predicted 0.70, and the halves overlap.
- **POOL.** 0.94 to 0.99 a head by attention (two in 1.90 undisturbed) for 0.97. The collision in the compressed part, +0.8, was met: the first two heads took 2.71 beside the shift, the next two 1.90, and the two beside the weighing 2.20.

```profile
437.50 2.71 POOL L1244 TENSOR_TENSOR work<-work,head_share 128x128 f32<-128x128 f32 x4 [50.06 <-DVE head_share L1192]
440.66 1.90 POOL L1244 TENSOR_TENSOR work<-work,head_share 128x128 f32<-128x128 f32 x4 [0.45 <-DVE head_share L1192]
```

- **Fourth attention.** 30.16 and 30.05 for 30.1, with the help of chance: the terms miss and cancel. From PE's transposes of the fourth and of the last head in the first trace:

```profile
799.02 0.55 PE L1054 MATMUL bank<-table,work 128*128 128x128 f32 x3 [0.38 <-POOL work L1244]
...
816.54 0.55 PE L1054 MATMUL bank<-table,work 128*128 128x128 f32 x3
```

  The start took 7.6 for 7.9, the three groups 17.5 for 18.3, and the end behind the last head's transposes 5.1 for 3.9: the last copy came later (3.6 until the values for 3.2), and the values ran at half clock (1.48 for 0.7). What holds that end, DVE's split ahead of the last copy, is confirmed by experiment 5.
- **Third attention.** 60.70 and 60.39 for 60.6, partly by chance: some of it is the half clock at 437 to 448, which I had priced by itself. Its end was 4.6 for 4.0.
- **The starts.** -1.7 and -2.3 were summed, -4.0 together; alone they measured -4.5. The fourth's share is smaller (-1.4 to -2.1 in the traces), the third's larger by what before lost to half clock there.
- **First attention.** +0.6 taken, bounds 0 and +1.5. The traces of the two kernels give +0.9, inside the bounds, but before's was at half clock for longer there (6.8 us, the changed kernel 3.4). The edit alone measured +2.6 [1.3, 3.9], above the term and just reaching into its bounds: the term most likely mis-sized, and the likely reason shows in the rows. I had the roots and POOL's 512-column steps beside them, and had seen in [rows 5] what the two do to each other, yet took the 3.27 of [rows 9] for the roots, which had only POOL steps of at most 0.48 beside them. They took 3.7, behind a copy that ended 0.4 later than I had it, and the first bias came at 100.4 where 99 to 100 stood. The longer wait of PE (3.6) was followed by a stretch at half clock, which was not in the term. Experiment 11, with no root ahead of the first bias, took 3.3 us out of this stage. The Trainium skill, page "SBUF — State Buffer", section "Who interferes with whom", says that a DVE instruction with two SBUF inputs and a GpSimd one that reads SBUF exclude each other. The row at 97.26 agrees, with 1.19 for 0.18.
- **Clock.** 0.4 was allowed for clock and mode switches together. The long executions reach 9 us over the shortest; in the one that has a trace most of the extra time lies in the tails of the two attentions (experiment 6), and filling PE's idle pieces took the half clock out of the loops (experiment 7). I had said single episodes +1 each; the measured difference of 3.8 is 2.7 more than that of the two first traces, and the allowance of 0.4 didn't cover it.
- **Sum.** First +2.6, starts -4.5, and by difference +5.7 for the two loops and clock (+5.3 by the stages of the traces): +3.8, where I had +2.2. The forecast, slower through the round, was right in its mechanism. By these numbers the first attention was 2 us short and the starts gave 0.5 back, but each of the parts has an interval of 1.1 us or more to either side, so how the missing 1.6 divides isn't shown. That the forecast of 1081.9 meets the median of 1081.88 is luck: it was added to a time before of 1079.68, a median of three, where 20 executions gave 1079.14, and by the ratio the change costs 3.8 and not 2.2.

## What to carry to other kernels

When work moves to a third engine in a loop whose engines run fixed orders, list every round that closes over the loop, not the engine's busy time; where several are close in length, cut none by itself but reorder all engines together (here 12 us by the order of ACT and DVE, 16 with two more moves, and no work removed). Look at what an engine's idle piece is followed by: a wait of 2 us ahead of a dense stretch can cost as much again through the clock (2.3 us behind the fourth attention in one long execution), and in other executions nothing. Small steps on DVE with two SBUF inputs belong where POOL is idle, or where DVE has time to spare.

## What was not expected of the hardware

Column halves overlapped in either order of the four matmuls, 0.80 and 0.81 us for a pair of heads against 0.67 for one. Keeping PE busy with transposes raised the granted clock to 1.00 through both attentions in experiment 7 and the longest of 12 executions was 1083.8, where the changed kernel had reached 1088.8 in 20; but rows of them placed ahead of dense work cost more than they gave (5 us in experiment 12). An idle piece of 1.8 us was followed by half clock in one execution and not in another of the same place. What makes the remaining spread of 6 us, which before had as well in the later rounds, stays open.
